# 24 feature units of 256-column products become 48 half units with one 512-column product for both activation parts

## The chip, the cores and the metric

The kernel runs on one core of one Trainium2 chip. The metric is the device time of one execution in microseconds (us), the median of several runs. Engines: PE is TensorE, DVE is VectorE, ACT is ScalarE, POOL is GpSimd, SP is the engine that issues nearly all DMAs.

## The reference, cut to what matters

Sequence 256, model width 2048, everything float32. A first block (pooling mixer and HGRN2, cross attention with a memory, mixture of experts) is followed by two layers of a hybrid block (mLSTM and RG-LRU). Nearly all the work is projections of 256 tokens by weights of 2048 rows:

```
proj = h @ w_in[l]                      # first block: u, q_in, f_in, i_in, g_in
u, q_in, f_in, i_in, g_in = jnp.split(proj, splits, axis=-1)
...
p = u @ w_in                            # each of the two layers of the second block
qk, v, o, z_a, ig, fg, xb, z_b = jnp.split(p, SPLIT_AT, axis=-1)
qk = jax.nn.silu(causal_dwconv(qk, qk_conv))
...
xc = causal_dwconv(xb, lru_conv_w) + lru_conv_b
y_b = rg_lru(xc, w_a, b_a, w_x, b_x, lam) * jax.nn.silu(z_b)
```

In `rg_lru` the gates are `sigmoid(xc @ w_a + b_a)` and `sigmoid(xc @ w_x + b_x)` per head; from them come `a = exp(log_a)`, the input `x * i * sqrt(1 - a*a)` and a linear recurrence over the sequence.

## The kernel before, in words

**Products in two parts.** PE multiplies in the type float32r. To keep float32 accuracy every operand is split into a high part (rounded to float32r) and a low part (the rest), and a product is the sum of three: high weights by high activations, high weights by low activations, low weights by high activations. Activations lie in `a_hi` and `a_lo` (and `b_hi`, `b_lo`), each 128 partitions x 16 k x 256 tokens. Weights are streamed: SP loads chunks of 1 MB into `raw` (4 slots, L520), ACT copies each half of a chunk to `w_hi` (L1379) and DVE subtracts to get `w_lo` (L1977). A "half" is 1024 weight values per partition. `w_hi` and `w_lo` have 4 slots each, so the weights of a half can be ready at most 4 halves ahead of PE: ACT writes the slot of half n when PE has finished half n-4 (semaphore `used`).

**Units.** A unit is 8 halves. In a feature unit (`mm_features`, L652 to L663) the weights are stationary and the result has features on partitions: per k and per 128 features three matmuls of 256 columns, so 24 matmuls per half, 192 per unit, for 512 features. In a token unit (`mm_tokens`) the activations are stationary and each matmul has 512 columns. A unit's result fills one of two buffers in PSUM, `pairs[:, 0]` and `pairs[:, 1]` (two banks each); unit u uses buffer u % 2 and waits until unit u-2 has been read (`pair_read`).

**Order by hand.** ACT and DVE run one hand-written list each. Between the steps of the weight stream (`run(1)` is one half) stand the other tasks. In the two layers this is a table: `m_` counts the units 0 to 15 of a layer and `todo[i]` holds the tasks that come before the i-th half of that unit (`todo[8]` after the last). The engines work in order, so a task that waits holds the weight stream behind it. The units of a layer in PE's order are 8 `lru` units (xb and z_b alternating, four pairs j = 0 to 3), 4 `qk` units, then token units.

**One pair in the steady state.** Call the halves of the even unit (xb of pair j+1, PE unit n = 2j+2) E0 to E7 and those of the odd unit (z_b) O0 to O7. PE computes the gates of pair j, whose products with `w_ax` are in plain float32 (`lru_gates`, L1128), in two parts, after E1 and after E2. Then ACT does the 8 sigmoids (`sigmoids`, L1792, `todo[8]` of the even unit), the weights of O0, then `exps` (L1800 to L1806), then the weights of O1. DVE does, in the odd unit, `gated_input`, `one_minus_a2` after O1, `pad_in` (reads the even unit out of PSUM, times a row of scales, into `XP`; L2572) after O2, convolution tile 0 after O3, `recur` (a product and 4 scans) after O4, convolution tile 1 after O5, `gated_output` after O6; in the next even unit `y_lo`, tiles 2 and 3 and `z_in` (reads the odd unit, L2572). A convolution tile is 4 instructions (L2622, L2628). In the fourth pair the even unit is the first `qk` unit; tiles go on through the `qk` units.

Of the kernel before, what the change touches and what calls it, by code (L numbers as in the profile page):

```python
# [5 lines left out]
ALU = mybir.AluOpType  # L6
# [85 lines left out]
def program(nc, t, out):  # L92
    with ExitStack() as ctx:
# [11 lines left out]
        a_hi = sb("a_hi", [P, KT, S], F32R)  # L105
        a_lo = sb("a_lo", [P, KT, S], F32R)
# [372 lines left out]
        for name, n in (("u", 2), ("f", 2), ("q", 2), ("i", 2), ("g", 2), ("mk", 4), ("mv", 4),  # L479
                        ("wout", 4), ("wq", 4), ("wo", 4), ("moe", 48)):  # L480
            stage(name, n)
# [15 lines left out]
        for l in range(LAYERS):  # L497
            for name, n in (("lru", 8), ("qk", 4), ("wb", 4), ("voz", 12), ("wa", 4)):
                stage(f"{name}{l}", n)
# [15 lines left out]
        def _(sp):  # L515
            def chunk(c, count, src):

                sp.wait_ge(hi_done, count)
                sp.wait_ge(lo_done, count)
                sp.dma_start(raw[:, c:c + 1] if len(src.shape) == 4 else raw[:, c], src).then_inc(landed[c], 16)  # L520
# [26 lines left out]
            units(H["f"], 2, w_in, F0)  # L547
            units(H["q"], 2, w_in, Q0)
# [48 lines left out]
            for l in range(LAYERS):  # L597
# [4 lines left out]
                for j in range(4):  # L602
                    units(H[f"lru{l}"] + 2 * j * HALVES, 1, w_in2[l], XB2 + j * COLS)
                    for c in range(CHUNKS):
                        if c == 1:

                            if l or j:
                                sp.wait_ge(gates_mm, 4 * l + j)
                            for m, name in enumerate(("w_a_2", "w_x_2")):
                                sp.dma_start(w_ax[:, m], t[name][l, 2 * j:2 * j + 2]  # L610
                                             .rearrange("h (k p) n -> p (h k) n", p=P))\
                                  .then_inc(wax_in, 16)
                        chunk(c, H[f"lru{l}"] + (2 * j + 1) * HALVES + 2 * c + 2,
                              w_in2[l][:, 4 * c:4 * c + 4, ZB2 + j * COLS:ZB2 + (j + 1) * COLS])
                units(H[f"qk{l}"], 4, w_in2[l], QK2)
# [24 lines left out]
        def _(pe):  # L640
# [38 lines left out]
            def pair_count(u):  # L679

                return u // 2 + PAIR_FREE

# [100 lines left out]
            for r in range(2):  # L783
                unit(pair_count(U["f"] + r), H["f"] + r * HALVES, r, mm_features, a_hi, a_lo,
                     hooks={i: (lambda c=2 * r + i // 4: turn(1, c, memx)) for i in (1, 5)})
            units("q", 2, mm_features, a_hi, a_lo)
# [426 lines left out]
            for l in range(LAYERS):  # L1213
                for n in range(8):
                    if n == 0 and l == 0:
                        continue
                    hooks = {1: lambda: turn_sum(5, 3, "wa0")} if n == 0 else {}
                    if n == 1:
                        hooks = {1: lambda: rows_out(l)}
                    if n >= 2 and n % 2 == 0:  # L1220
                        j = n // 2 - 1
                        hooks = {1: (lambda j=j: lru_gates(l, j, 0)), 2: (lambda j=j: lru_gates(l, j, 1))}
                    unit(pc(U[f"lru{l}"] + n), H[f"lru{l}"] + n * HALVES, n % 2, mm_features, a_hi,
                         a_lo, need=ready(4 + l) if n == 0 else {}, hooks=hooks)
                for n in range(4):
                    hooks = {}
                    if n == 0:
                        hooks = {1: lambda: lru_gates(l, 3, 0), 2: lambda: lru_gates(l, 3, 1)}
                    unit(pc(U[f"qk{l}"] + n), H[f"qk{l}"] + n * HALVES, n % 2, mm_features, a_hi,
                         a_lo, hooks=hooks)  # L1230
# [130 lines left out]
        def _(act):  # L1361
# [350 lines left out]
            def lru_unit(l, m_):  # L1712
# [109 lines left out]
                if 2 <= m_ <= 8 and m_ % 2 == 0:  # L1822
                    j = m_ // 2 - 1
                    todo[5].append(lambda: z_silu(j))
                    todo[8].append(lambda: sigmoids(j))
# [139 lines left out]
        def _(dve):  # L1965
# [130 lines left out]

            def features(dst, name, j, ready):

                u = by_row_x(dst[:, 4 * j:4 * j + 4, :], name, j)
                copied(dve, u)  # L2100
                v.sem_inc(ready, 1)
# [21 lines left out]
            pooled(1); run(3); split_lo(1, 0, b_hi, b_lo, "norm_mem"); run(1)  # L2123
# [20 lines left out]
            run(3); split_lo(1, 1, b_hi, b_lo, "norm_mem"); run(1); features(kb, "f", 0, f_in)  # L2144
            run(2); forget(0); run(1); split_lo(1, 2, b_hi, b_lo, "norm_mem"); run(1)
            run(1); decay_sums(0); run(2); split_lo(1, 3, b_hi, b_lo, "norm_mem"); run(1)
            features(kb, "f", 1, f_in); run(2); forget(1); run(2)
            run(1); decay_sums(1); run(1); lam_end(); run(2); features(qb, "q", 0, q_in); run(4)

# [41 lines left out]
            for l in range(LEVELS):  # L2191
                run(1)
                sub_odd(l)
                if l == 0:
                    run(3)
# [4 lines left out]
                else:  # L2200
# [22 lines left out]
            v.scalar_tensor_tensor(a_lo[:, 8:16, :].rearrange("p k t -> p (k t)"),  # L2223
                                   misc[:].rearrange("p b c -> p (b c)"), col("hgrn_norm"),
                                   a_hi[:, 8:16, :].bitcast(F32).rearrange("p k t -> p (k t)"),
# [348 lines left out]

            def pad_in(l, i):

                if i == 0:
                    dve.wait_ge(xp_zero, l + 1)
                if 8 * l + i:
                    dve.wait_ge(conv_ok, 8 * l + i)  # L2580
                m, u = by_row(XP[:, :, CONV_W - 1:], *((f"lru{l}", 2 * i) if i < 4 else (f"qk{l}", i - 4)))
                m.then_inc(pair_read[u % 2], 1)

            def z_in(l, j):

                if 4 * l + j:
                    dve.wait_ge(lru_lo, 4 * l + j)
                m, u = by_row(Zb, f"lru{l}", 2 * j + 1)
# [14 lines left out]
            def conv_tile(l, i, f):  # L2603
# [3 lines left out]
                if f == 0:  # L2607
                    if i < 4:
                        copied(dve, U[f"lru{l}"] + 2 * i)
# [4 lines left out]
                    else:  # L2614
                        copied(dve, U[f"qk{l}"] + i - 4)
# [10 lines left out]
                for w in range(1, CONV_W):  # L2626
# [3 lines left out]
                    if w < CONV_W - 1:  # L2630
# [145 lines left out]
            for l in range(LAYERS):  # L2776
                for m_ in range(16):
# [22 lines left out]
                    if m_ <= 7 and m_ % 2 == 1 or 9 <= m_ <= 12:  # L2800
# [5 lines left out]
                        todo[two].append(lambda i=i: conv_tile(l, i, 1))  # L2806
                    if 2 <= m_ <= 8 and m_ % 2 == 0 or 10 <= m_ <= 13:
                        i = m_ // 2 - 1 if m_ <= 8 else m_ - 6
                        todo[1].append(lambda i=i: conv_tile(l, i, 2))
                        todo[2].append(lambda i=i: conv_tile(l, i, 3))  # L2810
                    if 2 <= m_ <= 8 and m_ % 2 == 0:
                        todo[3].append(lambda: z_in(l, m_ // 2 - 1))
# [84 lines left out]
```

## Time and profile before

| | |
|---|---|
| median of 3 runs | 2974.2 us (2971.52 to 2974.97) |
| profiled execution, own time | 2976.89 us |
| its span | 2975.2 us |
| granted PE clock, mean | 0.997 |
| PE busy | 2931.8 us (99%) |
| DVE busy | 1935.3 us (65%) |
| ACT busy | 1649.4 us (55%) |
| DMA queue of the weights | 61.1% of 16 engines |

Matmul durations overlap in such a profile; the distance between starts is the cost of one. The busy shares are means over stages that differ.

### The profile page before, as it was taken

What the parts mean: (1) busy time and instruction counts of PE and PEld (TensorE: products, weight loads), DVE (VectorE), ACT (ScalarE), POOL (GpSimd) and SP (SyncE); (2) the same over time, 40 slices, a digit from 0 to 9 for tenths busy, and PEclk for the clock granted to TensorE, in tenths of its full rate; (3) what the DMA queues carried; (4) which work ended last, traced back from release to release, by engine and by line L of the source; (5) the groups of instructions that cost most, each with busy time, mean ns of one, the idle gap of its engine ahead of it and who ended that gap; (6) DMA issues with size and microseconds to landing.
All of it is one profiled execution on the core that took longest, in us unless ns stands there. A gap on an engine that the chain in (4) does not pass through costs nothing.

```text
span 2975.2 us, 41370 instructions
## 1 busy us (share of the span) xinstructions
PE 2931.8 (99%) x16792; PEld 2571.3 (86%) x16792; DVE 1935.3 (65%) x2265; ACT 1649.4 (55%) x1957; POOL 109.8 (4%) x87
## 2 busy tenths in 40 slices
PE   8999999999899999999999999999999999999998
PEld 8988988998777777777999988888899999888886
DVE  6767444535698989888676764555556677555554
ACT  6544444435587878777555544544545654444453
POOL 2222000000000000000000000000000000000000
PEclk9999999999999999999999999999999999999999
DMA  7545566645498989899555555555564545555553
GB/s 266 178 141 164 197 211 235 212 156 177 139 360 308 355 312 358 312 344 317 187 170 184 170 178 190 171 173 181 182 202 143 197 157 184 187 181 181 174 198 127
DMA packets 275545, 629.35 MB, mean 212 GB/s; under 512 B 18681, under 2 KB 28450, under 8 KB 258082
## 3 DMA queue, kind: packets, MB, share of 16 engines
q1 hardware_dynamic: 273890, 621.51, 61.1%
q10 hardware_dynamic: 1184, 4.20, 0.4%
q8 instruction: 133, 2.18, 0.3%
q0 software_dynamic: 288, 1.05, 0.1%
q14 instruction: 50, 0.41, 0.0%
HBM read 619.38 MB, written 7.34 MB: 211 GB/s over the span
## 4 chain that ended last, share of the span: by engine, by line
PE 83%; DVE 6%; issue 5%; ACT 4%; DMA 2%; SPq 0%; POOL 0%; POOLq 0%; ACTq 0%; DVEq 0%
PE pairs L647 17%; PE pairs L649 17%; PE pairs L648 17%; PE pairs L657 8%; PE pairs L659 8%; PE pairs L661 8%; DVE w_lo L1977 3%; PE misc L1128 2%; ACT w_hi L1379 1%; PE misc L806 1%; PE misc L1058 1%; PE misc L1014 1%; ACT scratch L1792 1%; DVE scratch L2658 1%; DMA raw<-in_w_down_dram 1%
## 5 line engine op out<-in xcount | busy, mean ns | idle before, releaser
L1977 DVE TENSOR_TENSOR w_lo<-raw,w_hi 128x1024 fp32r<-128x1024 f32 x1136 | 1386.2, 1242 | 861.8 <-ACT w_hi L1379 854.1
L1379 ACT ACTIVATE w_hi<-raw 128x1024 fp32r<-128x1024 f32 x1136 | 1183.0, 1059 | 955.7 <-PE pairs L649 581.8
L647 PE MATMUL pairs<-w_hi,a_hi 128*128 128x512 f32 x1664 | 659.1, 396 | 9.2 <-DVE w_lo L1977 5.6
L649 PE MATMUL pairs<-w_hi,a_lo 128*128 128x512 f32 x1664 | 648.4, 390 | 0.0
L648 PE MATMUL pairs<-w_lo,a_hi 128*128 128x512 f32 x1664 | 648.0, 389 | 0.0
L657 PE MATMUL pairs<-a_hi,w_hi 128*128 128x256 f32 x1920 | 551.1, 287 | 6.0 <-DVE w_lo L1977 6.0
L659 PE MATMUL pairs<-a_lo,w_hi 128*128 128x256 f32 x1920 | 544.2, 283 | 0.0
L661 PE MATMUL pairs<-a_hi,w_lo 128*128 128x256 f32 x1920 | 544.1, 283 | 0.0
L647 PEld LDWEIGHTS pairs<-w_hi,a_hi 128*128 128x128 f32 x1664 | 312.5, 188 | 83.3 <-DVE w_lo L1977 17.6
L657 PEld LDWEIGHTS pairs<-a_hi,w_hi 128*128 128x128 f32 x1920 | 369.1, 192 | 10.7 <-DVE w_lo L1977 6.9
L659 PEld LDWEIGHTS pairs<-a_lo,w_hi 128*128 128x128 f32 x1920 | 369.4, 192 | 0.7 <-issue 0.2
L649 PEld LDWEIGHTS pairs<-w_hi,a_lo 128*128 128x128 f32 x1664 | 312.4, 188 | 66.2
L661 PEld LDWEIGHTS pairs<-a_hi,w_lo 128*128 128x128 f32 x1920 | 369.2, 192 | 0.0
L648 PEld LDWEIGHTS pairs<-w_lo,a_hi 128*128 128x128 f32 x1664 | 312.6, 188 | 63.1 <-issue 0.7
L647 PE MATMUL pairs<-w_hi,b_hi 128*128 128x512 f32 x896 | 356.7, 398 | 1.8 <-DVE w_lo L1977 1.6
L649 PE MATMUL pairs<-w_hi,b_lo 128*128 128x512 f32 x896 | 349.1, 390 | 0.0
L648 PE MATMUL pairs<-w_lo,b_hi 128*128 128x512 f32 x896 | 348.9, 389 | 0.0
L647 PEld LDWEIGHTS pairs<-w_hi,b_hi 128*128 128x128 f32 x896 | 168.3, 188 | 40.7 <-issue 3.5
L648 PEld LDWEIGHTS pairs<-w_lo,b_hi 128*128 128x128 f32 x896 | 168.4, 188 | 36.4 <-issue 2.9
L649 PEld LDWEIGHTS pairs<-w_hi,b_lo 128*128 128x128 f32 x896 | 168.2, 188 | 35.6
L657 PE MATMUL pairs<-b_hi,w_hi 128*128 128x256 f32 x512 | 146.5, 286 | 0.0
L661 PE MATMUL pairs<-b_hi,w_lo 128*128 128x256 f32 x512 | 144.9, 283 | 0.0
(358 smaller groups left out, 2275.7 us busy)
## 6 DMA issues: line engine op xcount, KB each, us to landing
raw<-in_w_in_dram SPq DMA_DIRECT2D x232, 1024.0 KB, 5.2
raw<-in_w_out_dram SPq DMA_DIRECT2D x80, 1024.0 KB, 5.1
raw<-in_w_gate_dram SPq DMA_DIRECT2D x64, 1024.0 KB, 6.0
raw<-in_w_up_dram SPq DMA_DIRECT2D x64, 1024.0 KB, 6.2
raw<-in_w_down_dram SPq DMA_DIRECT2D x64, 1024.0 KB, 6.8
raw<-in_xattn_wk_dram SPq DMA_DIRECT2D x16, 1024.0 KB, 5.1
raw<-in_xattn_wv_dram SPq DMA_DIRECT2D x16, 1024.0 KB, 5.1
raw<-in_xattn_wq_dram SPq DMA_DIRECT2D x16, 1024.0 KB, 5.2
```

What stands on the lines that cost most here:

```text
L647: nc.tensor.matmul(o, hi[:, k, tok], w_hi[:, s, q, :], start=k == 0, stop=False)
L648: nc.tensor.matmul(o, hi[:, k, tok], w_lo[:, s, q, :], start=False, stop=False)
L649: m = nc.tensor.matmul(o, lo[:, k, tok], w_hi[:, s, q, :], start=False, stop=last)
L657: nc.tensor.matmul(o, w_hi[:, s, q, fs], hi[:, k, :], start=(k == 0 and f % 2 == 0), stop=False, skip_group_check=True)
L659: nc.tensor.matmul(o, w_hi[:, s, q, fs], lo[:, k, :], start=False, stop=False, skip_group_check=True)
L661: m = nc.tensor.matmul(o, w_lo[:, s, q, fs], hi[:, k, :], start=False, stop=last, skip_group_check=True)
L806: m = nc.tensor.matmul(misc[:, 2 * T + h // 4, (h % 4) * P:(h % 4 + 1) * P], a[:, h, tok], b[:, h, tok], start=True, stop=True)
L1014: m = nc.tensor.matmul(o, x_rows[:, T, 4 * c + k, :], pick[:, T, 0:tiles * P], start=T == 0, stop=T == TT - 1)
L1058: m = nc.tensor.matmul(misc[:, 2 + T, :], place[:, s, T * P:(T + 1) * P], y_out[:, s, :], start=s == 0, stop=s == tiles - 1)
L1128: m = nc.tensor.matmul(misc[:, 2 * m_ + a, f * S:(f + 1) * S], w_ax[:, m_, 2 * a + k, f * P:(f + 1) * P], xc[:, 2 * a + k, :], start=k == ...
L1379: a.activation(w_hi[:, i % HSLOTS], raw[:, i // 2, 2 * (i % 2):2 * (i % 2) + 2, :], ACT.Copy).then_inc(hi_done, 1)
L1977: v.tensor_tensor(w_lo[:, i % HSLOTS], raw[:, i // 2, 2 * (i % 2):2 * (i % 2) + 2, :], w_hi[:, i % HSLOTS].bitcast(F32), ALU.subtract).the ...
```

## The change

The high and low activations lie side by side (`a_both`), so one 512-column matmul with the high weights gives both products; the low weights still take a 256-column matmul. The result of 128 features then needs a whole bank (high sum | low sum), so a buffer holds 256 features: 24 of the 30 feature units on `a` (2 of f, 2 of q, and per layer 6 `lru` and 4 `qk` units) become 48 narrow units of 4 halves. DVE adds the two parts while it reads (`tensor_reduce`), and multiplies by the row afterwards in SBUF. Weight chunks of narrow units have rows of 1 KB instead of 2 KB. The gates move from after E1 and E2 to after E3 and E4; tile 1 moves from the odd unit to `todo[1]` of the next even one, with tiles 2 and 3 one step later, and `z_in` from `todo[3]` to `todo[4]`, `z_silu` from `todo[5]` to `todo[6]`.

```diff
-        a_hi = sb("a_hi", [P, KT, S], F32R)
-        a_lo = sb("a_lo", [P, KT, S], F32R)
+        a_both = sb("a_both", [P, KT, 2, S], F32R)
+        a_hi, a_lo = a_both[:, :, 0, :], a_both[:, :, 1, :]
...
+            def narrow_unit(u, h, r, both, hooks):
+
+                pe.wait_ge(pair_read[r], u)
+                for i in range(HALVES // 2):
+                    pe.wait_ge(lo_done, h + (RAW_FREE + i + 1))
+                    wh, wl = (z[:, i].rearrange("p a (b n) -> p (a b) n", b=2) for z in (w_hi, w_lo))
+                    for q in range(4):
+                        k = 4 * i + q
+                        for f in range(2):
+                            o = pairs[:, r, f, :]
+                            fs = slice(f * P, (f + 1) * P)
+                            nc.tensor.matmul(o, wh[:, q, fs], both[:, k].rearrange("p w t -> p (w t)"),
+                                             start=k == 0, stop=False, skip_group_check=True)
+                            m = nc.tensor.matmul(o[:, 0:S], wl[:, q, fs], both[:, k, 0, :], start=False,
+                                                 stop=k == KT - 1, skip_group_check=True)
+                    m.then_inc(used, 1)
+                    if i in hooks:
+                        hooks[i]()
...
-                        hooks = {1: (lambda j=j: lru_gates(l, j, 0)), 2: (lambda j=j: lru_gates(l, j, 1))}
+                        hooks = {3: (lambda j=j: lru_gates(l, j, 0)), 4: (lambda j=j: lru_gates(l, j, 1))}
...
+            def add_narrow(dst, name, n):
+
+                u = U[name] + n
+                finished(dve, H[name] + (n + 1) * (HALVES // 2))
+                v.tensor_reduce(dst, pairs[:, u % 2].rearrange("p f (w t) -> p f t w", w=2), AX.X, ALU.add)\
+                 .then_inc(pair_read[u % 2], 1)
...
+            def by_r_row(z):
+
+                return v.tensor_tensor(z, z, r_row.unsqueeze(1).to_broadcast([P, 4, S]), ALU.mult)
...
+                if i:
+                    u = pad_part(l, i, 1)
+                    copied(dve, u - 1)
+                    copied(dve, u)
+                    step(by_r_row(XP[:, :, CONV_W - 1:]))
+                    return
...
                         todo[one].append(lambda i=i: conv_tile(l, i, 0))
-                        todo[two].append(lambda i=i: conv_tile(l, i, 1))
...
+                        if i > 3:
+                            todo[two].append(lambda i=i: conv_tile(l, i, 1))
                     if 2 <= m_ <= 8 and m_ % 2 == 0:
-                        todo[3].append(lambda: z_in(l, m_ // 2 - 1))
+                        for f in range(1, 4):
+                            todo[f].append(lambda i=m_ // 2 - 1, f=f: conv_tile(l, i, f))
...
+                    if 2 <= m_ <= 8 and m_ % 2 == 0:
+                        todo[4].append(lambda: z_in(l, m_ // 2 - 1))
...
+                    if 4 <= m_ <= 8 and m_ % 2 == 0:
+                        todo[0].append(lambda: z_part(l, m_ // 2 - 1, 0))
+                    if m_ in (2, 4, 6, 8, 9, 10, 11):
+                        todo[7].append(lambda: pad_part(l, m_ // 2 if m_ <= 6 else m_ - 4, 0))
```

In the first block `sum_f` reads the narrow units of f and q in the same way (one reduce each), and `features` multiplies by the row afterwards; the last one, `sum_f(qb, "q", 3)`, stands just before `features(qb, "q", 1, q_in)` and one half of weights.

## Rows read from the trace of the kernel before

**Rows 1.** The page, part 1: busy us, share of the span, instructions.

```profile
PE 2931.8 (99%) x16792; PEld 2571.3 (86%) x16792; DVE 1935.3 (65%) x2265; ACT 1649.4 (55%) x1957; POOL 109.8 (4%) x87
```

**Rows 2.** Groups by line and form: busy us, mean ns, idle before them and its releaser.

```profile
L2572 DVE TENSOR_TENSOR scratch<-pairs,scratch 128x1024 f32<-128x1024 f32 x24 | 29.3, 1220 | 1.3 <-PE pairs L661 1.2
```

**Rows 3.** Timeline of PE, feature unit: start us, us; first and last of 31 starts.

```profile
60.09 0.28 PE L657 MATMUL pairs<-a_hi,w_hi 128*128 128x256 f32 x1
...
63.69 0.28 PE L657 MATMUL pairs<-a_hi,w_hi 128*128 128x256 f32 x1
```

**Rows 4.** Timeline of PE, token unit: first and last of 13 starts.

```profile
200.45 0.39 PE L647 MATMUL pairs<-w_hi,a_hi 128*128 128x512 f32 x1
...
203.17 0.39 PE L647 MATMUL pairs<-w_hi,a_hi 128*128 128x512 f32 x1
```

**Rows 5.** Windows: us; busy PE, PEld, DVE, ACT, POOL; PE clock, DMA share, GB/s.

```profile
1510.32:1540.24 29.92, 29.92 (x226) 29.09 (x225) 14.06 (x16) 17.69 (x27) 0.00 (x0) 1.00 0.52 186
1540.24:1564.40 24.16, 23.66 (x194) 23.19 (x193) 22.12 (x28) 13.85 (x14) 0.00 (x0) 1.00 0.50 160
1648.40:1672.44 24.04, 23.58 (x194) 23.18 (x193) 22.03 (x27) 13.85 (x14) 2.14 (x2) 1.00 0.50 159
...
115.04:138.08 23.04, 23.04 (x195) 23.04 (x193) 18.23 (x28) 13.90 (x13) 2.78 (x1) 1.00 0.54 172
```

**Rows 6.** Timeline of PE, one pair: starts of E3, E4, O0 and O5.

```profile
1525.67 0.47 PE L657 MATMUL pairs<-a_hi,w_hi 128*128 128x256 f32 x1
...
1528.72 0.28 PE L657 MATMUL pairs<-a_hi,w_hi 128*128 128x256 f32 x1
...
1540.24 0.28 PE L657 MATMUL pairs<-a_hi,w_hi 128*128 128x256 f32 x1
...
1555.52 0.38 PE L657 MATMUL pairs<-a_hi,w_hi 128*128 128x256 f32 x1 [0.50 <-DVE w_lo L1977]
```

**Rows 7.** Timeline of ACT, same pair: weights of E7, sigmoids, weights of O1 to O3.

```profile
1528.92 1.06 ACT L1379 ACTIVATE w_hi<-raw 128x1024 fp32r<-128x1024 f32 x1 [5.21 <-PE pairs L661]
...
1531.29 3.03 ACT L1792 ACTIVATE scratch<-misc,vecs 128x256 f32<-128x256 f32 x8
...
1540.89 2.94 ACT L1379 ACTIVATE w_hi<-raw 128x1024 fp32r<-128x1024 f32 x3
```

**Rows 8.** Timeline of DVE: weights of O1, O5, tile 1, weights of O6.

```profile
1541.96 1.23 DVE L1977 TENSOR_TENSOR w_lo<-raw,w_hi 128x1024 fp32r<-128x1024 f32 x1 [4.30 <-ACT w_hi L1379]
...
1554.27 1.19 DVE L1977 TENSOR_TENSOR w_lo<-raw,w_hi 128x1024 fp32r<-128x1024 f32 x1
1555.39 0.40 DVE L2622 TENSOR_SCALAR scratch<-scratch,vecs 128x256 f32<-128x256 f32 x1
...
1557.28 1.22 DVE L1977 TENSOR_TENSOR w_lo<-raw,w_hi 128x1024 fp32r<-128x1024 f32 x1
```

**Rows 9.** Groups by form: a strided read, a plain read, a reduce.

```profile
L1594 ACT ACTIVATE scratch<-x 128x512 f32<-128x512 f32 x8 | 8.4, 1110 | 0.1
...
L2268 DVE TENSOR_REDUCE small<-misc 128x2 f32<-128x512 f32 x4 | 2.8, 693 | 22.0 <-PE misc L879 22.0
...
L1648 ACT ACTIVATE scratch<-misc 128x512 f32<-128x512 f32 x4 | 2.4, 598 | 0.0
```

**Rows 10.** DMA issues: count, KB each, median us from issue to landing.

```profile
raw<-in_w_in_dram SPq DMA_DIRECT2D x232, 1024.0 KB, 5.2
...
scratch<-in_w_x_dram SPq DMA_DIRECT2D x8, 512.0 KB, 5.6
```

**Rows 11.** Timeline at the start of the i units, DVE, ACT and PE.

```profile
164.94 1.21 DVE L2087 TENSOR_TENSOR scratch<-pairs,scratch 128x1024 f32<-128x1024 f32 x1
...
165.21 1.28 ACT L1474 ACT_TABLE_LOAD   x1
...
166.50 1.06 ACT L1474 ACTIVATE scratch<-scratch 128x1024 f32<-128x1024 f32 x1
...
167.61 3.84 PE L806 MATMUL misc<-scratch 128*128 128x128 f32 x32 [0.86 <-ACT scratch L1474]
```

More of the change, by code:

```diff
@@ L497, in program @@
         for l in range(LAYERS):
-            for name, n in (("lru", 8), ("qk", 4), ("wb", 4), ("voz", 12), ("wa", 4)):
+            stage(f"lru{l}", 2)
+            stage(f"narrow{l}", 12, HALVES // 2)
+            stage(f"qk{l}", 8, HALVES // 2)
+            for name, n in (("wb", 4), ("voz", 12), ("wa", 4)):
                 stage(f"{name}{l}", n)
@@ L519, in chunk, with narrow, narrow_units @@
                 sp.wait_ge(lo_done, count)
-                sp.dma_start(raw[:, c:c + 1] if len(src.shape) == 4 else raw[:, c], src).then_inc(landed[c], 16)
+                to = raw[:, c]
+                if src.shape[-1] == S:
+                    to = to.rearrange("p a (b n) -> p (a b) n", b=2)
+                sp.dma_start(to, src).then_inc(landed[c], 16)
+            def narrow(h0, view, first):
+                for c in range(CHUNKS):
+                    at = first + c // 2 * S
+                    chunk(c, h0 + 2 * c + 2, view[:, 8 * (c % 2):8 * (c % 2) + 8, at:at + S])
+            def narrow_units(h0, n, view, first):
+                with sp.Fori(0, n) as j:
+                    for c in range(CHUNKS):
+                        chunk(c, j * HALVES + (h0 + 2 * c + 2),
+                              view[:, 8 * (c % 2):8 * (c % 2) + 8, bass.ds(j * COLS + (first + c // 2 * S), S)])
             def units(h0, n, view, first):
@@ L602, in _ @@
                 for j in range(4):
-                    units(H[f"lru{l}"] + 2 * j * HALVES, 1, w_in2[l], XB2 + j * COLS)
+                    h0 = H[f"lru{l}"] + 2 * j * HALVES
+                    if j:
+                        narrow(h0, w_in2[l], XB2 + j * COLS)
+                    else:
+                        units(h0, 1, w_in2[l], XB2)
                     for c in range(CHUNKS):
@@ L681, in pair_count, with narrow_pair @@
                 return u // 2 + PAIR_FREE
+            def narrow_unit(u, h, r, both, hooks):
[15 more added lines that the diff above has]
+                        hooks[i]()
+            def narrow_pair(u, h, both, hooks={}):
+                for r in range(2):
+                    narrow_unit(pair_count(u + r), h + r * (HALVES // 2), r, both,
+                                {i - 4 * r: f for i, f in hooks.items() if i // 4 == r})
             def units(name, n, body, hi, lo, need={}):
@@ L782, in _ @@
             unit(pair_count(U["u"] + 1), H["u"] + HALVES, 1, mm_features, a_hi, a_lo, hooks={0: row_x_out})
[L783 to L786, printed above, removed]
+            for n in range(2):
+                narrow_pair(U["f"] + 2 * n, H["f"] + n * HALVES, a_both,
+                            hooks={i: (lambda c=2 * n + i // 4: turn(1, c, memx)) for i in (1, 5)})
+            for n in range(2):
+                narrow_pair(U["q"] + 2 * n, H["q"] + n * HALVES, a_both)
             def level(l):
@@ L1221, in _ @@
                         j = n // 2 - 1
[L1222 to L1224 removed]
+                        hooks = {3: (lambda j=j: lru_gates(l, j, 0)), 4: (lambda j=j: lru_gates(l, j, 1))}
+                    if n < 2:
+                        unit(pc(U[f"lru{l}"] + n), H[f"lru{l}"] + n * HALVES, n % 2, mm_features, a_hi,
+                             a_lo, need=ready(4 + l) if n == 0 else {}, hooks=hooks)
+                    else:
+                        narrow_pair(U[f"narrow{l}"] + 2 * (n - 2), H[f"lru{l}"] + n * HALVES, a_both, hooks)
                 for n in range(4):
@@ L2194, in _ @@
                 if l == 0:
-                    run(3)
+                    run(2)
+                    sum_f(qb, "q", 3)
+                    run(1)
                     dve.wait_ge(pooled_out, 32)
@@ L2607, in conv_tile @@
                 if f == 0:
+                    if i:
+                        step.wait()
                     if i < 4:
-                        copied(dve, U[f"lru{l}"] + 2 * i)
+                        if i == 0:
+                            copied(dve, U[f"lru{l}"])
                         if 4 * l + i:
```

98 lines of the change are left out of this document (61 added, 37 removed).

## The prediction, made before the changed kernel was run

> **What bounds the kernel now.** I read the page first: PE is busy for 99% of the span, DVE for 65% [rows 1]. That alone says little, since matmul durations overlap; the cost of a product is the distance between starts. In a feature unit 30 products of 256 columns take 63.69 - 60.09 = 3.60 us, 0.1200 each [rows 3]; in a token unit 12 products of 512 columns take 203.17 - 200.45 = 2.72, 0.2267 each [rows 4]. At 2.4 GHz (the granted clock is 1.00 in the windows) these are 288 and 544 cycles: 256 + 32 and 512 + 32. Each product with its own weight load pays 32 cycles, 13.3 ns, on top of its columns. A feature unit of 192 products takes 23.04 us if nothing stalls, as the q unit does [rows 5].
>
> Then I asked which feature units stall. The window of an even lru unit takes 29.92 us: 23.04 and 6.88 for two gate parts. The odd unit after it takes 24.16, 1.12 too many, with DVE busy for 22.12 of it; the first odd qk unit 24.04 [rows 5]. So the even unit has room and the odd one has none. The timelines show why. ACT works without a break from the weights of E7 through sigmoids and exps to the weights of O1 (1528.92 to 1540.89), so DVE waits 4.30 us and starts the weights of O1 at 1541.96, 1.72 after PE began O0 [rows 6 to 8]. From there DVE runs without a break to the weights of O5 at 1554.27, 12.31 later, and PE starts O5 1.25 after that [rows 6, 8]. Both chains of this odd unit matter, ACT's and DVE's: this is where the change is decided.
>
> **The gain.** Per k and 128 features, three products of 256 columns (0.360 us) become one of 512 and one of 256 (0.3467): the same 768 columns, one weight load fewer, 13.3 ns. 24 units x 64 such groups = 1536, times 13.3 ns = 20.5 us, 0.853 per unit; a half takes 2.773 instead of 2.88. I take the whole of it: both spacings are measured with the load in them, and there is no reason for more than that. The lower bound of the gain is nothing. The Trainium skill, TensorE: Matmul & The Clock Gate, section Back-to-back issue gap, gives an isolated gap of N/2.4 + 2.5 ns; by it one product fewer would be worth 2.5 ns and the whole 3.8 us. Rows 3 and 4 show 32 cycles and not 6, so the rows decide.
>
> **What DVE gets.** Before, one read of 1024 elements from PSUM, 1.22 us [rows 2]. Now two reduces of 1024 elements to 512 and one multiplication in SBUF. The trace has no such reduce. The reduce from PSUM of 512 elements takes 0.693 [rows 9] and the product of 1024 takes 1.22; 512 elements more for 0.53 us is 1.03 ns each, one element per DVE cycle, so the reduce of 1024 would take 1.22, started 1.13 apart (1.26 where the next waits for its result). But its inner step jumps by 256 elements. The only row with such jumps, an ACT copy with steps of 16 elements, takes 1.110 where a plain one of the same size takes 0.598 [rows 9]: about 1.0 ns more per element. With that a reduce takes 2.3. These are the two ends. I take 1.22, since operation, engine and memory are those of the reduce row, and keep 2.3 for the range. Extra at 1.22: 2.4 us per unit, 58 us of DVE in all. In the f and q units it is hidden: DVE is busy for 18.23 of 23.04 [rows 5], 20.7 of 22.2 after, and has up to four halves of lead.
>
> **The odd unit after the change.** Let T be the start of E5, right after the second gate part, which now lies behind E4. Of E5, E6, E7 the weights are ready.
> - ACT: it sees PE's signal some 0.20 after (1528.72 to 1528.92), I take 0.25. The table load no longer costs its 1.28: ACT loads a table before it waits (the load at 165.21 begins while DVE's product it waits for still runs [rows 11]). From the first sigmoid to the weights of O1: 1540.89 - 1531.29 = 9.60 [rows 7]. So the high part of O1 begins at T + 9.85, the low part 1.07 later at T + 10.92, PE can begin O1 1.28 later, at T + 12.20. PE wants it at 4 x 2.773 + 0.17 (the first half after a gate is that much longer) = T + 11.26. Stall 0.94.
> - DVE: from the weights of O1 to those of O5 12.31 before; now one dependent reduce more in `pad_in`, 1.26, so 13.57: T + 24.49. PE begins O5 at T + 25.76. Without stalls it would be 8 x 2.773 + 0.17 = T + 22.35. So 3.41 in all, against 1.12 before: 2.29 more. Tile 1 is gone from behind O5 (1555.39 to 1557.28, 1.89 [rows 8]), which makes O6 safe but comes too late for O5.
> - The next even unit: DVE has `y_lo`, one reduce, three tiles and four halves. Counted on, the weights of E0 to E3 are ready 1.3, 1.1, 0.8 and 0.6 before PE wants them. No stall, little room. `z_in` then falls beside the first gate part, `conv_ok` is there 5 us before the gate.
> - The fourth pair keeps its tile 1 (i = 4) and gets `pad_part` after O6 and a two-step `pad_in` three halves later. Same counting: 3.35, then 0.2, 0.6 and 0.6: 4.8 against 1.01, 3.8 more.
>
> Per layer 3 x 2.29 + 3.8 = 10.7, two layers 21.3 us.
>
> **The rest.** At the i units PE waits for `q_ok` (0.86 before the level products [rows 11]). Before `features` stand now a reduce and its wait: 1.15 more, and nothing hides it. DMA: 1 MB in rows of 1 KB (the two gate weights, issued together) lands within 5.6 us, a chunk of 2 KB rows in 5.2 [rows 10]; a chunk has at least 4 halves = 11 us. The gate weights and the chunk of O2 are held until the gates are done (SP waits for `gates_mm`), which is now nearer to O2: issued at T + 0.4 and T + 1.4, landed by about T + 11.4, wanted by ACT at T + 10.8 and by DVE at T + 13.2. I cost it at nothing; if every one came 2 us later than DVE wants it, 6 pairs x 2 = 12 us. The copies of activations into `a_both` cost as before.
>
> **Sum.** -20.5 + 21.3 + 1.15 = +2.0 us. Against its own 2976.9 the profiled execution would become 2978.9; the median lies 2.7 lower, so 2976 to 2977. I say 2976.5: no change that can be told.
>
> **Rivals.**
> - A, the forecast: the gain is eaten by the odd units. 2976.5, own range 2969 to 2985, chance 0.52. The tight places (0.6 to 1.3 us) can only add.
> - B, the strided reduce takes 2.3. In each pair one such reduce lies in DVE's chain (1.1 more for O1 to O5) and one before the tight even unit (0.4 after its room): 4.9 of stalls per pair, 3.8 over before. The fourth has three in tight places: about 9, 7.9 over. Layers 2 x (3 x 3.8 + 7.9) = 38.6; i units 2.2; q some 2. -20.5 + 42.8 = +22: 2997. For it speaks the only strided row, against it that this row is another engine and memory. Chance 0.32. The Trainium skill, Advanced Engine Details and Errata, section Memory Cachelines, says that PSUM has lines of 8 bytes and that every two consecutive elements should be contiguous; it says so of matmuls. By it every element of this reduce is a new line. No row here shows it for DVE.
> - C, faster: DVE and ACT keep their timing to PE, because DVE has 4.30 us idle before the weights of O1 [rows 8] and the additions fall there. Stalls stay 1.12 per pair: -20.5 + 1.15, 2955. Against it: the work of the odd unit is in order behind the weights of O1 and can't go into that gap. It decides from an extra of under 1.9 us per pair. Chance 0.10.
> - D, the chunk of O2 comes late behind the gate weights: +12, 2989 (chance 0.06).
>
> **How the numbers follow.** The bound for telling a change is 0.2%, 6 us: below 2968.3, above 2980.2. Slower: 0.14 of A's 0.52, B's 0.32, D's 0.06, 0.52 in all. Same: 0.36, from A. Faster: 0.02 of A and 0.10 of C, 0.12. Range 2966 to 3001: A and most of B and D, not C and not the top of B.
>
> **What the profile after would show.** Starts 0.347 apart per pair of products, 2.77 per half: if not, the gain is mis-sized. The reduce's mean: 1.22 is A, 2.3 is B; this row decides most. Odd windows of 22.2 + 3.4, even ones 22.2 + 6.9; the fourth odd one longer. Wrong would be the prediction if O1's weights were not late, if even units stalled, or if ACT's idle named the DMA of `raw`.

## The result: slower by 0.3%

| | before | after |
|---|---|---|
| median | 2974.99 us (7 runs, 2971.52 to 2977.98) | 2983.5 us (7 runs, 2982.77 to 2985.67) |
| span of the profiled execution | 2975.2 us | 2981.3 us |

The ratio is 1.0029, 95% interval 1.0019 to 1.0038: slower, by 8.5 us. The forecast was 2976.5 with a range of 2966 to 3001. The time lies in the range, but 7 us above the point, and the point said that no change could be told, where one can. The chance of 0.52 for slower came mostly from rivals B and D, which did not happen (below); account A alone gave it 0.14.

The page after, part 1, which answers to [rows 1]: 1536 matmuls fewer, and 53 us more of DVE. (Durations of DVE add up to 57.9 us more, as forecast with 58; the page counts overlapping ones once.)

```profile
PE 2918.5 (98%) x15256; PEld 2482.9 (83%) x15256; DVE 1988.0 (67%) x2313; ACT 1649.9 (55%) x1957; POOL 109.9 (4%) x87
```

Groups of DVE instructions after, by line and form (busy us, mean ns, idle before them). These two are the new work, the reduce and the multiplication in SBUF (four more multiplications belong to f and q):

```profile
L2158 DVE TENSOR_REDUCE scratch<-pairs 128x512 f32<-128x1024 f32 x48 | 58.5, 1219 | 1.5 <-PE pairs L725 0.9
...
L2648 DVE TENSOR_TENSOR scratch<-scratch 128x1024 f32<-128x1024 f32 x20 | 24.5, 1226 | 2.1
```

The reduce takes 1.219 us, as long as the plain read of 1024 elements from PSUM [rows 2], so its step of 256 elements costs DVE nothing that shows: rival B's price of 2.3 is out.

Windows after, columns as in [rows 5]: the even unit E, the odd unit O, the second qk unit, the first q unit, and the fourth qk unit of layer 0 and of layer 1.

```profile
1506.94:1536.40 29.46, 29.46 (x162) 25.66 (x161) 17.63 (x21) 16.95 (x26) 0.00 (x0) 1.00 0.37 114
1536.40:1562.13 25.73, 23.33 (x131) 19.54 (x129) 22.94 (x27) 14.62 (x15) 0.00 (x0) 1.00 0.77 237
1646.61:1673.29 26.68, 23.85 (x131) 19.50 (x129) 23.74 (x29) 14.66 (x16) 1.64 (x2) 1.00 0.46 134
113.28:135.47 22.19, 22.19 (x131) 19.41 (x129) 19.95 (x28) 13.90 (x13) 2.52 (x1) 1.00 0.58 191
1697.10:1719.71 22.61, 22.61 (x130) 19.60 (x129) 21.97 (x31) 9.56 (x9) 0.00 (x0) 1.00 0.64 206
2480.76:2502.95 22.19, 22.19 (x131) 19.41 (x129) 21.52 (x32) 9.55 (x9) 0.00 (x0) 1.00 0.65 202
```

The q unit shows the whole gain: 22.19 us for 23.04, DVE busy for most of it and never late. The odd unit lost 1.57 us instead (24.16 to 25.73), the second qk unit 2.63 (24.05 to 26.68). The last two rows are the same work, with nothing late in either, and differ by 0.42 us at the same granted clock; more on this below.

Cutting both traces at the starts of the units gives the account of the two executions:

| part | forecast | measured |
|---|---|---|
| f and q, 4 units | -3.4 | -3.3 |
| first i unit | +1.15 | +1.04 |
| 8 even units (gates) | -6.8 | -4.9 |
| 6 odd lru units | +8.6 | +10.5 |
| qk units 2 to 4, two layers | +2.5 | +5.3 |
| start, last wo unit, experts (the change alters only where the activations lie) | 0 | -2.5 |
| sum | +2.0 | +6.1 |

The window of the experts alone lasts 602.7 to 610.2 us in the profiles of this study, without order by kernel. Of the -2.5, -0.7 stands in the last wo unit, where the granted clock was at its lower level (0.50 of full speed) for 10.2 us before and for 6.8 after; the rest has no cause that I found. A single execution is therefore good to a few us. The windows of the units are steadier: the six odd lru units of before agree to 0.02 us, those of after to 0.30. With that row left out the change costs 8.6, close to the 8.5 between the medians.

The stalls themselves, from the timeline of PE after (the odd unit of the windows above; [rows 6] has its O0 and O5):

```profile
1536.40 0.40 PE L723 MATMUL pairs<-a_both,w_hi 128*128 128x512 f32 x1
...
1540.08 0.50 PE L723 MATMUL pairs<-a_both,w_hi 128*128 128x512 f32 x1 [0.70 <-DVE w_lo L2034]
...
1553.70 0.50 PE L723 MATMUL pairs<-a_both,w_hi 128*128 128x512 f32 x1 [1.58 <-DVE w_lo L2034]
```

These are O0, O1 and O5. The timeline of DVE after, same unit, answers to [rows 8]:

```profile
1538.80 1.22 DVE L2034 TENSOR_TENSOR w_lo<-raw,w_hi 128x1024 fp32r<-128x1024 f32 x1 [4.30 <-ACT w_hi L1436]
1539.94 1.22 DVE L2743 SCALAR_TENSOR_TENSOR scratch<-scratch 128x1024 f32<-128x1024 f32 x1
1541.08 1.22 DVE L2034 TENSOR_TENSOR w_lo<-raw,w_hi 128x1024 fp32r<-128x1024 f32 x1
1542.21 1.22 DVE L2158 TENSOR_REDUCE scratch<-pairs 128x512 f32<-128x1024 f32 x1
1543.54 1.23 DVE L2648 TENSOR_TENSOR scratch<-scratch 128x1024 f32<-128x1024 f32 x1
...
1548.84 1.22 DVE L2760 TENSOR_TENSOR scratch<-scratch 128x1024 f32<-128x1024 f32 x1
1550.09 2.44 DVE L2763 TENSOR_TENSOR_SCAN scratch<-scratch 128x256 f32<-128x256 f32 x4
1552.45 2.33 DVE L2034 TENSOR_TENSOR w_lo<-raw,w_hi 128x1024 fp32r<-128x1024 f32 x2
```

From the weights of O1 (1538.80) to those of O5 (1552.45) DVE has no gap: 13.65 us, before 12.31. Ahead of the weights of O1 it still idles 4.30 us for ACT. And ACT after:

```profile
1528.12 3.03 ACT L1849 ACTIVATE scratch<-misc,vecs 128x256 f32<-128x256 f32 x8 [6.98 <-PE misc L1183]
...
1537.72 2.94 ACT L1436 ACTIVATE w_hi<-raw 128x1024 fp32r<-128x1024 f32 x3
```

The first row is the sigmoids, 0.39 us behind T = 1527.73 (the start of E5), the second the weights of O1, O2 and O3 without a pause between them: the chunk of O2 had landed. In the lru and qk units of both layers no wait of ACT or DVE names a DMA, and O5 begins 25.93 to 25.97 us behind T in all six pairs: rival D did not happen.

### The profile page after: what moved, and what is told of

Read it like the earlier page. It is cut to its first block, busy times and chain, and to the rows that moved or that the text cites. A ratio compares the mean times of both kernels' runs of the same rounds, so it can differ in the third digit from the quotient of the medians.

```text
span 2981.3 us, 38403 instructions
## 1 busy us (share of the span) xinstructions
PE 2918.5 (98%) x15256; PEld 2482.9 (83%) x15256; DVE 1988.0 (67%) x2313; ACT 1649.9 (55%) x1957; POOL 109.9 (4%) x87
## 4 chain that ended last, share of the span: by engine, by line
PE 82%; DVE 7%; issue 5%; ACT 4%; DMA 1%; SPq 0%; POOL 0%; POOLq 0%; ACTq 0%; DVEq 0%
PE pairs L676 17%; PE pairs L678 17%; PE pairs L677 17%; PE pairs L723 7%; DVE w_lo L2034 4%; PE pairs L686 4%; PE pairs L690 4%; PE pairs L688 4%; PE pairs L725 4%; PE misc L1183 2%; ACT w_hi L1436 1%; PE misc L861 1%; PE misc L1113 1%; PE misc L1069 1%; ACT scratch L1849 1%
## 5 line engine op out<-in xcount | busy, mean ns | idle before, releaser
L676 PE MATMUL pairs<-w_hi,a_both 128*128 128x512 f32 x1664 | 658.9, 396 | 9.5 <-DVE w_lo L2034 5.4
L678 PE MATMUL pairs<-w_hi,a_both 128*128 128x512 f32 x1664 | 648.4, 390 | 0.0
L677 PE MATMUL pairs<-w_lo,a_both 128*128 128x512 f32 x1664 | 648.1, 389 | 0.0
L723 PE MATMUL pairs<-a_both,w_hi 128*128 128x512 f32 x1536 | 547.3, 400 | 21.7 <-DVE w_lo L2034 21.2
L725 PE MATMUL pairs<-a_both,w_lo 128*128 128x256 f32 x1536 | 428.5, 279 | 0.0
L676 PEld LDWEIGHTS pairs<-w_hi,a_both 128*128 128x128 f32 x1664 | 312.4, 188 | 83.5 <-DVE w_lo L2034 16.9
L723 PEld LDWEIGHTS pairs<-a_both,w_hi 128*128 128x128 f32 x1536 | 288.2, 188 | 100.4 <-DVE w_lo L2034 31.7
L678 PEld LDWEIGHTS pairs<-w_hi,a_both 128*128 128x128 f32 x1664 | 312.3, 188 | 66.2
L677 PEld LDWEIGHTS pairs<-w_lo,a_both 128*128 128x128 f32 x1664 | 312.6, 188 | 63.1 <-issue 0.7
L725 PEld LDWEIGHTS pairs<-a_both,w_lo 128*128 128x128 f32 x1536 | 289.4, 188 | 0.4
L688 PE MATMUL pairs<-b_lo,w_hi 128*128 128x256 f32 x512 | 144.8, 283 | 0.0
L686 PE MATMUL pairs<-a_both,w_hi 128*128 128x256 f32 x384 | 110.8, 289 | 2.6 <-DVE w_lo L2034 2.6
```

The source lines that it names most:

```text
L676: nc.tensor.matmul(o, hi[:, k, tok], w_hi[:, s, q, :], start=k == 0, stop=False)
L677: nc.tensor.matmul(o, hi[:, k, tok], w_lo[:, s, q, :], start=False, stop=False)
L678: m = nc.tensor.matmul(o, lo[:, k, tok], w_hi[:, s, q, :], start=False, stop=last)
L686: nc.tensor.matmul(o, w_hi[:, s, q, fs], hi[:, k, :], start=(k == 0 and f % 2 == 0), stop=False, skip_group_check=True)
L688: nc.tensor.matmul(o, w_hi[:, s, q, fs], lo[:, k, :], start=False, stop=False, skip_group_check=True)
L723: nc.tensor.matmul(o, wh[:, q, fs], both[:, k].rearrange("p w t -> p (w t)"), start=k == 0, stop=False, skip_group_check=True)
```

## The experiments

Each kernel was timed beside the kernel before (4 to 11 executions). Ratios are to that kernel, with 95% intervals; the medians of before were 2973.9 to 2976.4, so medians of two experiments compare to 2 or 3 us only.

**wide_moves.** The schedule of the change without its products: all units wide, gates after E3 and E4, tile 1 and `z_in` moved.

```diff
-                        hooks = {1: (lambda j=j: lru_gates(l, j, 0)), 2: (lambda j=j: lru_gates(l, j, 1))}
+                        hooks = {3: (lambda j=j: lru_gates(l, j, 0)), 4: (lambda j=j: lru_gates(l, j, 1))}
...
+                        for f in range(1, 4):
+                            todo[f].append(lambda i=m_ // 2 - 1, f=f: conv_tile(l, i, f))
```

> The kernel before with the moves alone: gates after E3 and E4, tile 1 in the next even unit, z_in and z_silu one step later; all units stay wide. My reckoning by steps (the loss is DVE's new work, not the moves): weights of O1 ready at T + 12.2 against 11.7 wanted, weights of O5 at T + 24.5 against 23.2, so 1.3 us of stalls per pair against 1.12: 2976.5, within 1.5 of before. Rival, the moves cost most of what was lost (the gates' new place makes both chains late): 2983 or more.

Measured: 2977.92, ratio 1.0009 (1.0000 to 1.0018). The odd units last 24.53 to 24.55 us for 24.16, with waits at O1 and at O5. The moves cost some 3 us (by the layers' windows 3.3, while the interval of the ratio spans 0 to 5); the rest of the 8.5, 5 us, is narrow units on top of them, their gain included. The reckoning by steps said 1.5 for the moves, too little by half, and its rival, 2983 or more, is out.

**fq_only.** Narrow units in f and q, the layers as before.

> Narrow units in f and q alone, the two layers as before. By steps: four units x 0.85 gained, 1.04 lost at the i units: 2.4 us faster than before, 2972.6, and the layers' windows as before to 0.1 us. Rival, narrow units cost something everywhere (layout, DMA rows of 1 KB): not faster than 2975.

Measured: 2974.63, ratio 1.0002 (0.9993 to 1.0011): the gain of 2.4 us is not there. The layers' windows agree with those of before to 0.02 us, so the new layout of the activations costs nothing there, and the f and q units, with DMA rows of 1 KB, gained 3.3, nearly all of the 3.4 forecast. But the first i unit lasts 36.44, where it lasts 34.81 after and 33.77 before. The windows show where the time went (part of the level products; the clock is the third value from the end):

```profile
164.30:165.30 1.00, 0.96 (x8) 0.96 (x9) 0.00 (x0) 0.93 (x1) 0.00 (x0) 1.00 0.97 360
165.30:168.40 3.10, 3.10 (x17) 3.10 (x17) 0.00 (x0) 0.00 (x0) 0.00 (x0) 0.52 0.48 185
```

```profile
164.34 5.47 PE L850 MATMUL misc<-scratch 128*128 128x128 f32 x32 [1.89 <-ACT scratch L1518]
```

After a wait of 1.89 us PE starts its 32 products at 2.4 GHz, and then the granted clock falls to the lower level, 1.2 GHz, for 3.1 us. The products take 5.47 us where they take 3.84 in the run after, behind the same wait. So 1.6 us, half of what f and q won, is lost again in this execution; why the clock fell is not shown.

**fq_half.** To shorten that wait: tiles 4 and 5 of q are multiplied one half earlier.

```diff
-                    run(2)
+                    run(1)
+                    copied(dve, U["q"] + 2)
+                    z = qb[:, 4:6, :]
+                    v.tensor_tensor(z, z, row_x.unsqueeze(1).to_broadcast([P, 2, S]), ALU.mult)
+                    run(1)
                     sum_f(qb, "q", 3)
```

> fq_only with the multiplication of the last q unit in two parts: tiles 4 and 5 one half earlier, so that behind the last reduce only 512 elements (some 0.69 us) stand in place of 1024 (1.22). If DVE's chain behind the last q unit sets the start of the level products, PE waits 1.36 us there for 1.89 and the window of the first i unit is 34.3 where it was 34.8 in the run after and 36.4 in fq_only, where the granted clock fell behind this wait. If the length of the wait brings the fall on, it won't show here: 2972.5. Rival, the wait stays (something else is late) and the fall comes by chance: 2974.6.

Measured: 2973.43, ratio 1.0007 (0.9988 to 1.0026). One of the eleven executions took 3002.63 at a mean granted clock of 0.937, where the others had 0.995 to 0.997; it widens the interval and lifts the ratio above 1, though the median is 0.4 below that of before. Nothing of the order of 1 us can be told from it. The windows show more: the wait is 1.36 as counted, the first i unit 34.28, and in this execution the clock stays up.

```profile
164.09 3.84 PE L850 MATMUL misc<-scratch 128*128 128x128 f32 x32 [1.36 <-ACT scratch L1518]
```

**after_g23.** The changed kernel with the gates one half earlier.

```diff
-                        hooks = {3: (lambda j=j: lru_gates(l, j, 0)), 4: (lambda j=j: lru_gates(l, j, 1))}
+                        hooks = {2: (lambda j=j: lru_gates(l, j, 0)), 3: (lambda j=j: lru_gates(l, j, 1))}
```

(and the same for the first qk unit)

> The changed kernel with the gates after E2 and E3 (one half earlier than it has them, one later than before). If the odd unit's stalls come from ACT's and DVE's chains that start at the second gate part: with T' the start of E4, O1 is ready at T' + 12.4 and wanted at 14.0, O5 at T' + 25.9 and wanted at 25.1, so 0.8 us of stalls per pair for 3.7: 8 x 2.9 = 23 us less, 2960. Rival, DVE's amount of work in the odd unit is the bound wherever the gates stand: only the stall at O1 goes, 8 x 1.06, 2975.

Measured: 2961.57, ratio 0.9955 (0.9941 to 0.9969), 22 us less than after. The wait at O1 is gone, the one at O5 is down from 1.58 to 0.64; even unit, then odd unit:

```profile
1505.39:1534.53 29.14, 29.14 (x162) 25.50 (x161) 18.10 (x22) 19.65 (x29) 0.00 (x0) 1.00 0.47 148
1534.53:1557.62 23.09, 22.45 (x130) 19.38 (x129) 22.70 (x27) 12.14 (x12) 0.00 (x0) 1.00 0.73 225
```

DVE does the same list of work as after in an odd unit that is 2.64 us shorter. Its amount was not the bound; its start was. (With 22.70 us busy of 23.09 the amount is close to being one now.) The idle time of DVE before the weights of O1 is as long as ever, but it ends before PE starts O0 at 1534.53:

```profile
1534.30 1.22 DVE L2034 TENSOR_TENSOR w_lo<-raw,w_hi 128x1024 fp32r<-128x1024 f32 x1 [4.30 <-ACT w_hi L1436]
```

**before_g23.** The same edit in the kernel before: {1, 2} to {2, 3}.

> The kernel before with the gates after E2 and E3, nothing else. By the same steps the stalls of 1.12 us in the odd units and of 1.0 in the first odd qk unit go: 8 x 1.1 = 9 us less than before, 2966. Rival, the gates' products find conv_ok later or ACT waits as long as before: 2975.

Measured: 2964.95, ratio 0.9966 (0.9952 to 0.9979). Every odd unit lasts 23.04, none stalls. So of the three places tried, the middle one, which neither kernel had, is the best (narrow units were not run with the first). After E1 and E2, ACT waits for E3 to be done before it may write E7's weights and come to the sigmoids [rows 7]: they start 2.57 us behind the start of E4, 5.6 behind the end of the second gate part. After E3 and E4 they start 0.39 behind the second gate part (that in the run after), but that part stands a half later in the unit. After E2 and E3 they start 0.39 behind it too (E4 begins at 1522.33), since E7's weights are made while it runs. ACT in this kernel, the weights of E7 and the sigmoids:

```profile
1519.27 1.06 ACT L1379 ACTIVATE w_hi<-raw 128x1024 fp32r<-128x1024 f32 x1 [5.20 <-PE pairs L661]
...
1522.72 3.03 ACT L1792 ACTIVATE scratch<-misc,vecs 128x256 f32<-128x256 f32 x8 [1.10 <-PE misc L1128]
```

**after_2red.** The second reduce of `pad_in` is done twice, its result unchanged.

```diff
+                if part:
+                    finished(dve, H[name] + (n + 1) * (HALVES // 2))
+                    step(v.tensor_reduce(XP[:, 2:4, CONV_W - 1:],
+                                         pairs[:, (U[name] + n) % 2].rearrange("p f (w t) -> p f t w", w=2),
+                                         AX.X, ALU.add))
+                    step.wait()
```

> The changed kernel with the second reduce of pad_in done twice, 1.26 us of DVE more before the weights of O4 in each odd unit and in the qk units. If DVE's chain sets the start of O5, each of the eight stalls there grows by 1.26, 10 us, and the third qk units by as much, 2.5: 2996. Rival, the reduce isn't on the path that sets O5 (ACT or the transfers are): 2983.5 to 2986.

Measured: 2995.68, ratio 1.0068 (1.0055 to 1.0082): 12.2 us more than after. The op stands in 14 places; by the windows ten of them, the odd lru units and the second and third qk units, grow by 1.1 to 1.5 each, and the other four by next to nothing. The timeline of PE, an odd unit (O1, O3 and O5):

```profile
1540.52 0.51 PE L723 MATMUL pairs<-a_both,w_hi 128*128 128x512 f32 x1 [0.70 <-DVE w_lo L2034]
...
1547.65 0.50 PE L723 MATMUL pairs<-a_both,w_hi 128*128 128x512 f32 x1 [1.21 <-DVE w_lo L2034]
...
1555.40 0.50 PE L723 MATMUL pairs<-a_both,w_hi 128*128 128x512 f32 x1 [1.62 <-DVE w_lo L2034]
```

The sum is as expected, the place is not: the wait at O5 is no longer than after (1.62 for 1.58); the added op shows at O3, since `pad_in` stands before the weights of O3 and not of O4. In this unit a delay of DVE is paid where the next weights are due, and all later ones shift with it.

**after_order.** Products of a k in the order 512, 512, 256, 256 columns.

```diff
                         for f in range(2):
-                            o = pairs[:, r, f, :]
-                            fs = slice(f * P, (f + 1) * P)
-                            nc.tensor.matmul(o, wh[:, q, fs], both[:, k].rearrange("p w t -> p (w t)"),
+                            nc.tensor.matmul(pairs[:, r, f, :], wh[:, q, f * P:(f + 1) * P],
+                                             both[:, k].rearrange("p w t -> p (w t)"),
                                              start=k == 0, stop=False, skip_group_check=True)
-                            m = nc.tensor.matmul(o[:, 0:S], wl[:, q, fs], both[:, k, 0, :], start=False,
+                        for f in range(2):
+                            m = nc.tensor.matmul(pairs[:, r, f, 0:S], wl[:, q, f * P:(f + 1) * P],
```

> The changed kernel with the four products of a k in the order 512, 512, 256, 256 columns (256-column products of low weights last) in place of 512, 256, 512, 256. In the trace after, halves without a stall last 2.77 us or 2.83 and keep one of the two values until PE has stalled. If the alternation of the two lengths makes this slower pattern, all free halves last 2.77 here and some 2 to 3 us go: 2981. Rival, the pattern comes from something else (where PE takes up after a stall, the buffer of PSUM): both values stay, 2983.5.

Measured: 2984.96, ratio 1.0027 (1.0017 to 1.0038), no different from after. In the trace the two values are gone, but the one that came is neither of them: every free half (one in which PE waits for nothing) lasts 2.79, a fourth qk unit 22.29 in both layers.

```profile
1701.94:1724.23 22.29, 22.29 (x130) 19.45 (x129) 21.62 (x32) 9.57 (x9) 0.00 (x0) 1.00 0.64 204
```

By windows the layers lose 9.5 us to before, where after lost 10.8. So the slow pattern goes with the alternation, and the fast one too; the median can't show a gain of 1 us.

**after_g23_r6.** after_g23, with `recur` (3.6 us) behind the weights of O5 in three pairs of four.

```diff
-                        todo[5].append(lambda j=j: recur(l, j))
+                        todo[6 if j < 3 else 5].append(lambda j=j: recur(l, j))
```

> The changed kernel with the gates after E2 and E3 and recur (3.6 us of DVE) behind the weights of O5 in place of before them, in three of four pairs. If DVE's chain from O1 to O5 is what is left of the stall, O5 is ready before PE wants it and O6 too (start of its low part at T' + 25.7, wanted 26.6): six stalls of 0.9 less than with the gates moved alone (2961.6), 2956. Rival, the stall only moves on to O6 or O7 or the next even unit: 2961.

Measured: 2955.89, ratio 0.9935 (0.9922 to 0.9949). All six odd lru units are free of stalls (four last 22.19, two 22.62 in the slow pattern), this one with DVE busy for all but 0.32 us of it:

```profile
1531.40:1553.59 22.19, 22.19 (x131) 19.41 (x129) 21.87 (x25) 12.02 (x12) 0.00 (x0) 1.00 0.73 224
```

**best.** More of the same in the second and third qk unit, and fq_half's edit.

```diff
-                        todo[7].append(lambda j=j: gated_output(l, j))
+                        todo[7 if j < 3 else 8].append(lambda j=j: gated_output(l, j))
...
+                        if i == 5:
+                            todo[4].append(lambda: step(by_r_row(XP[:, :, CONV_W - 1:])))
                         if i > 3:
-                            todo[two].append(lambda i=i: conv_tile(l, i, 1))
+                            todo[7 if i == 4 else two].append(lambda i=i: conv_tile(l, i, 1))
```

> after_g23_r6 and the rest of the list: recur behind O5 in the fourth pair too, tile 1 there after O6, gated_output after O7, y_lo of the fourth pair at todo[6] of the third qk unit, the multiplication of pad_in(5) one half later, and the last q unit's multiplication in two parts. By the chain of DVE from O1 on, the 3.1 us of stalls in the second and third qk unit of a layer come down to 0.4: 5.4 us in two layers and 0.5 at the i units less than the 2955.9 of after_g23_r6, 2950. Rival, the work only comes due later (fourth qk unit or wb): 2955.

A miss: 2959.53, ratio 0.9949 (0.9936 to 0.9963). The two units last 48.5 us together, 0.8 more than in after_g23_r6 (1.0 in layer 1). That is 1.9 of the 3.6 us between the two medians; the rest does not show in the profile, which is the fastest of the five executions. The timelines of ACT and DVE at the start of the third qk unit:

```profile
1654.64 1.06 ACT L1871 ACTIVATE b_hi<-scratch 128x1024 fp32r<-128x1024 f32 x1 [8.73 <-DVE scratch L2760]
1655.60 3.88 ACT L1436 ACTIVATE w_hi<-raw 128x1024 fp32r<-128x1024 f32 x4
```

```profile
1656.68 1.23 DVE L2034 TENSOR_TENSOR w_lo<-raw,w_hi 128x1024 fp32r<-128x1024 f32 x1 [2.07 <-ACT w_hi L1436]
```

I had counted DVE's work and not who waits for it. `y_hi` stands in ACT's list ahead of the next weights and waits for `gated_output`; moved one step later on DVE, it made ACT wait until 1654.64 (8.73 us) with four weight copies behind it, and DVE then waited 2.07 for the first of them.

**best2.** best with `y_hi` of the fourth pair two halves later in ACT's list, and `y_lo` in the fourth qk unit.

```diff
-                    todo[8].append(lambda: y_hi(j))
+                    if j < 3:
+                        todo[8].append(lambda: y_hi(j))
+                if m_ == 10:
+                    todo[2].append(lambda: y_hi(3))
```

> As best, but ACT's y_hi of the fourth pair stands before the third half of the third qk unit in place of before the first (in best it waited there for the moved gated_output and held ACT's copies of weights), and y_lo in the fourth qk unit. If that hold made the stalls of 1.76 and 1.06 us that best has in the second and third qk unit, these units last 44.4 to 45.2 us together in place of 48.5 (47.7 in after_g23_r6): 2.5 us per layer less than after_g23_r6, 2950. Rival, DVE's amount of work before the end of the third qk unit is the bound: 47 us or more together, 2955.

Measured: 2952.62, ratio 0.9913 (0.9896 to 0.9931), the fastest kernel of the study, 24 us below the before of its comparison and 31 below the changed kernel. Second and third qk unit, layer 0 and layer 1:

```profile
1636.89:1659.54 22.65, 22.65 (x130) 19.59 (x129) 22.23 (x28) 11.81 (x12) 0.00 (x0) 1.00 0.53 156
1659.54:1681.73 22.19, 22.19 (x131) 19.57 (x129) 21.57 (x33) 11.21 (x13) 0.00 (x0) 1.00 0.68 198
2405.42:2428.27 22.85, 22.46 (x130) 19.39 (x129) 22.43 (x28) 12.01 (x12) 0.00 (x0) 1.00 0.52 155
2428.27:2450.46 22.19, 22.19 (x131) 19.40 (x129) 21.57 (x33) 11.21 (x13) 0.00 (x0) 1.00 0.65 198
```

They last 44.84 and 45.04 us together, inside the 44.4 to 45.2 expected. Part of the work only came due later: the fourth qk unit, now with `y_lo`, waits 0.51 us for weights of DVE and lasts 23.31 and 23.05, where the one of after had no wait. Over the three units after_g23_r6 took 70.3 us in layer 0 and best2 takes 68.2.

## Why the prediction held, and where it was off

**The gain is there.** A free half lasts 2.77 us for 2.88, which is 0.85 per unit; both q units show it whole. So a product fewer was worth the 13.3 ns read from the rows, and the 3.8 us that the prediction set beside its 20.5 are out. Where free halves last 2.83 the gain is 0.4 per unit.

**The reduce.** 1.219 us, as taken from the row of the same operation; the strided ACT row was the wrong neighbour. The rule of the Trainium skill on memory cachelines (Advanced Engine Details and Errata), by which each element of this reduce would be a new line, is about matmuls, and DVE does not follow it here.

**The odd unit.** This step carried the prediction, and its mechanism is right: O1's weights are late, O5 is later, the even units do not stall, and ACT's idle time never names a DMA. From T the high part of O1 begins at 9.99 (forecast 9.85), its low part at 11.07 (10.92), PE begins O1 at 12.35 (12.20) and O5 at 25.97 (25.76). The sigmoids came 0.39 behind T where 0.25 was taken, and DVE's stretch to O5 took 13.65 for 13.57. That in this order T is what matters, and not the amount of DVE's work, is shown by after_g23; that DVE's chain is the path from O1 on, by after_2red and after_g23_r6.

**The terms that were too small**, 6.6 us in the layers by the table above:
- Even units: -0.62 each in the mean where -0.85 was forecast, 1.9 us in eight. In two of them all free halves last 2.77, and they gain 0.78; the two gate parts cost 6.95 there and not 6.88. The others hold halves of 2.82 or 2.83, a pattern that I did not know of.
- Odd units: 25.90 in the mean for 25.6, again 1.9 us in six. O5 is 0.19 later behind T than counted, in the mean of the six; 0.07 of that falls into the even unit, 0.12 into the odd one. 0.1 is the half after a stall, which is that much longer (2.88 where free ones last 2.77): the first two products of O1 start at 1540.08 and 1540.41, 0.33 apart where such starts are 0.23 apart later in the half. The trace of before shows a longer half too (3.02 for 2.88 behind its stall at O5), and I had not priced it. The rest, 0.08, is the slow pattern.
- Second to fourth qk unit: 6.5 and 5.9 us over three free units, for the 4.8 forecast; 2.8 in two layers. I had the O5 stall (3.5 for 3.35, in all). The later lateness is 1.7 for the 1.4 counted, and I missed that each stall makes the half behind it 0.1 to 0.2 longer, 0.7 per layer; in layer 0 another 0.7 is the slow pattern, in twelve halves.

**The i units**: 1.04 for 1.15 in this execution. That the clock can fall there, which cost 1.6 us in three of the profiles, was no part of the forecast.

**The rivals.** B is out by the reduce's row. D is out by ACT's timeline and the waits. C is out as well: DVE's 4.30 us before the weights of O1 were still there after, unused, as I held against it. They are there in after_g23 too; that kernel is as fast as C said only in part (2961.57 for 2955), and not because the additions fell into the gap, but because both chains start earlier. The moves alone cost 3 us and narrow units another 5 in that order; with the gates after E2 and E3 narrow units are faster than wide ones, by 3.4 us in the medians (2961.57 to 2964.95, five executions each, with intervals that overlap) and by 5.9 in the windows of the layers, f, q and the first i unit. best2 lies 23.8 below its before, and before_g23 10.1 below its own, some 14 us between them.

**What stays open**: what chooses between 2.77 and 2.83 after a stall, why the half after a stall is longer, when the clock falls at the first i unit, and what moves the experts' window by up to 7.5 us.

## What to carry to other kernels

When a cheaper product is paid for with work on another engine, don't compare busy shares: take the stage with the least room, name one event as zero, and count each engine's chain from it to the weights that PE wants next. If the chain starts late, move its start first: placing the gates well was worth 10 us to the kernel before and 22 to the changed one, and only then did the cheaper products pay. When an instruction is moved on one engine, look up who waits for it on the others, and what is queued behind that wait.

## What the runs showed of the hardware

- 512- and 256-column products in turn have two stable spacings at the same granted clock of 1.00: 0.347 us per two products, or 0.353. Starts of the slow one repeat over three pairs as 0.350, 0.350 and 0.360. In these traces a run of halves keeps its value until PE is held up or other products come between: the fourth qk unit of after had 22.61 in one layer and 22.19 in the other. In best2 a delay of 0.1 us between the second and third qk unit was enough to change it. Ordered 512, 512, 256, 256, there is one value, 0.348.
- A reduce on DVE from PSUM of 1024 float32 elements, added in pairs that lie 256 elements apart, takes 1.219 us, where a read of 1024 elements in order took 1.220 [rows 2]. An ACT copy with a step of 16 took 1.110 where a plain one took 0.598 [rows 9]; the first reads SBUF and the second PSUM, so the step is not shown to be the only cause.
- The half after a stall of 0.5 to 1.6 us lasts 0.1 to 0.2 us longer than a free one, at the same granted clock of 1.00.
- At the first i unit the granted clock fell to the 1.2 GHz level for some 3 us in three of the six profiles with a wait of 1.86 to 1.89 us before it (fq_only, after_g23_r6, after_2red), and in none of the six with a wait of 0.86 or 1.36. That is too few to call it a rule.
